# Two attention layers of a fused kernel: output products of heads in pairs, branch steps at set heads, rotation and projection started elsewhere

## What is computed

```python
h = modulate(rmsnorm(x), ...);  z = h @ w_in
q = rope(rmsnorm(z_q) @ w_q_b)                     # 8 heads of 64 + 32 (rotated)
k, v = ...rmsnorm(z_kv) @ w_kv_b...                # context keys first, then tokens
attn = softmax(q k^T / sqrt(96)) v                 # tokens: 512 keys; context: its own 256
conf = silu(layernorm(conv31(a * sigmoid(g)) + b)) # conformer branch, 256 channels
sc   = b_gate * conv3(c_gate * h_gate)             # short convolution branch, 256 channels
y = concat(rmsnorm(attn), rmsnorm(conf), rmsnorm(sc)) @ w_o
x = x + m2 * rmsnorm(y)
x = x + m5 * rmsnorm(relu(h2 @ w1)^2 @ w2)         # h2: modulated x
```

## Time and profile before

| | us |
|---|---|
| median of 3 runs | 1877.29 (1873.92 to 1880.47) |
| the profiled execution, its own time | 1874.17 |
| span of its trace | 1872.4 |
| PE busy | 1680.8 (90%) |
| DVE busy | 1229.1 (66%) |
| ACT busy | 483.0 (26%) |
| POOL busy | 467.5 (25%) |
| granted TensorE clock, mean | 0.955 of full |

### The profile page before, as it was taken

How to read it: one execution, slowest core, us unless ns; L and a number is a source line. 1 busy time by engine, 2 the same in 40 slices (tenths; PEclk the granted TensorE clock), 3 DMA queues, 4 the chain that set the end, 5 groups by cost and what they waited for, 6 DMA issues and landing times.

```text
span 1872.4 us, 26961 instructions
## 1 busy us (share of the span) xinstructions
PE 1680.8 (90%) x10862; PEld 1435.7 (77%) x10862; DVE 1229.1 (66%) x1658; ACT 483.0 (26%) x994; POOL 467.5 (25%) x368
## 2 busy tenths in 40 slices
PE   6888689999787999979988979999999788989997
PEld 6776489999676999958744748888888475679996
DVE  7752458887876888759774364444444696568886
ACT  3323221111351211142345251111011424531111
POOL 2300124443223344312100302121212130134442
PEclk9999799999998999989998989999999898999998
DMA  7445555554465655653200203233323141035561
GB/s 264 147 149 178 226 191 181 179 179 147 168 233 196 203 180 182 186 191 102 83 8 0 81 21 113 90 101 90 100 92 99 35 135 45 22 103 179 177 177 51
DMA packets 69874, 247.26 MB, mean 132 GB/s; under 512 B 7456, under 2 KB 10528, under 8 KB 69664
## 3 DMA queue, kind: packets, MB, share of 16 engines
q1 hardware_dynamic: 69792, 246.18, 40.6%
HBM read 245.10 MB, written 1.05 MB: 131 GB/s over the span
## 4 chain that ended last, share of the span: by engine, by line
PE 60%; DVE 28%; issue 5%; ACT 5%; POOL 1%; DMA 1%; SPq 0%; DVEq 0%; POOLq 0%; ACTq 0%
PE psum L318 13%; PE psum L319 13%; PE psum L320 13%; DVE lo_ring L293 9%; DVE relu L1048 4%; PE psum L334 3%; DVE hid_lo L1050 3%; PE psum L336 3%; PE psum L335 3%; PE psum L1362 2%; DVE c_conf L1592 2%; PE psum L908 1%; DVE x L1012 1%; PE psum L1386 1%; POOL hi_ring L1819 1%
## 5 line engine op out<-in xcount | busy, mean ns | idle before, releaser
L1819 POOL TENSOR_SCALAR hi_ring<-raw_ring 128x1024 fp32r<-128x1024 f32 x364 | 467.3, 1287 | 1377.9 <-PE psum L320 676.5
L293 DVE TENSOR_TENSOR lo_ring<-raw_ring,hi_ring 128x1024 fp32r<-128x1024 f32 x364 | 549.7, 1513 | 95.3 <-POOL hi_ring L1819 62.4
L318 PE MATMUL psum<-x_hi,hi_ring 128*128 128x256 f32 (+1 forms) x1440 | 453.0, 315 | 22.5 <-DVE lo_ring L293 22.5
L319 PE MATMUL psum<-x_lo,hi_ring 128*128 128x256 f32 (+1 forms) x1440 | 447.7, 311 | 0.0
L320 PE MATMUL psum<-x_hi,lo_ring 128*128 128x256 f32 (+1 forms) x1440 | 447.4, 311 | 0.0
L318 PE MATMUL psum<-hid_hi,hi_ring 128*128 128x256 f32 (+1 forms) x1024 | 315.7, 308 | 4.1 <-DVE hid_lo L1050 4.1
L320 PE MATMUL psum<-hid_hi,lo_ring 128*128 128x256 f32 (+1 forms) x1024 | 313.8, 306 | 0.0
L319 PE MATMUL psum<-hid_lo,hi_ring 128*128 128x256 f32 (+1 forms) x1024 | 313.2, 306 | 0.0
L318 PEld LDWEIGHTS psum<-x_hi,hi_ring 128*128 128x128 f32 x1440 | 278.1, 193 | 42.1 <-DVE lo_ring L293 27.4
L319 PEld LDWEIGHTS psum<-x_lo,hi_ring 128*128 128x128 f32 x1440 | 278.1, 193 | 14.2 <-issue 0.2
L320 PEld LDWEIGHTS psum<-x_hi,lo_ring 128*128 128x128 f32 x1440 | 277.8, 193 | 13.8
(11 more groups left out here) (353 smaller groups left out, 1837.8 us busy)
## 6 DMA issues: line engine op xcount, KB each, us to landing
raw_ring<-weights SPq DMA_DIRECT2D x460, 512.0 KB, 3.6
h_const<-hyb_consts SPq DMA_DIRECT2D x1, 1088.0 KB, 11.7
x<-xT SPq DMA_DIRECT2D x1, 1024.0 KB, 6.0
x<-ctxT SPq DMA_DIRECT2D x1, 1024.0 KB, 17.2
outT<-x SPq DMA_DIRECT2D x1, 1024.0 KB, 4.8
shared<-shared_consts SPq DMA_DIRECT2D x1, 398.0 KB, 13.8
par<-params SPq DMA_DIRECT2D x1, 301.5 KB, 6.6
```

Of the source, the lines that this page charges most:

```text
L293: nc.vector.tensor_tensor(lo_ring[:, u % SPLIT_SLOTS, :], raw_ring[:, UNIT_AT[u] % RAW_SLOTS, :], hi_ring[:, u % SPLIT_SLOTS, :].bitcast(F ...
L318: nc.tensor.matmul(bank(u % BANKS, T), w_hi, hi[:, k, 0:T], start=(k == 0), stop=False)
L319: nc.tensor.matmul(bank(u % BANKS, T), w_hi, lo[:, k, 0:T], start=False, stop=False)
L1819: nc.gpsimd.tensor_scalar(hi_ring[:, u % SPLIT_SLOTS, :], raw_ring[:, slot, :], 1.0, 0.0, ALU.mult, ALU.add).then_inc(hi_ready, 1)
```

## The change

Five edits, all in block 2's layers (and one constant that block 1's output projection reads as well).

1. **Heads in pairs.** `out_of(i)` is gone. `out_pair(i)` runs after `scores` in every even iteration for heads i-2 and i-1 together: for each key block one matmul of the even head (partitions 0 to 63), then one of the odd head (partitions 64 to 127), one signal for both. The number of matmuls and their shapes stay. `c_pT` gets four buffers (`c_pT_low`, `c_pT_high`; the second lies over `c_kv`, `c_kr` and `c_q`). DVE's `pair_out` moves one iteration later.
2. **Branch steps per engine.** `PE_STEPS`, `ACT_STEPS` and `DVE_STEPS` name, for each layer, the iterations at which each engine does its steps. PE does them at the head of iteration i as before; ACT and DVE now at its end. The flag `branch_sq` is split in `conf_sq` and `sc_sq`, ACT's `rstd` step in `rstd` and `sc_rstd`, DVE's `silu` step in `scaled` and `sc`. All taps that are left are done in iteration 0.
3. **Early rotation.** The first four rotation matmuls stand in the middle of the last query unit (after its second head) and not behind it; DVE's `rotate(0)` stands ahead of the last six taps of the unit phase and not behind them.
4. **Projection.** `LATE_FIRST` is [6, 7, 4, 5, 0, 1, 2, 3]: the short branch's blocks come first. PE's sum of the attention's squares stands between blocks 7 and 4.
5. **The end on ACT and DVE.** ACT squares three attention blocks, waits for the last output pair, then splits blocks 6, 7, 4, 5 and squares the fourth block among them.

```diff
-    LATE_FIRST = [4, 5, 6, 7, 0, 1, 2, 3]
+    LATE_FIRST = [6, 7, 4, 5, 0, 1, 2, 3]
...
-    STEPS = ["conf_mean", "center", "sums", "rstd", "silu", "again", "last"]
+    PE_STEPS = [{2: ["mean"], 4: ["sums"], 6: ["sc"], 8: ["again"]}, {1: ["mean"], 3: ["sums"], 4: ["sc"], 7: ["again"]}]
+    ACT_STEPS = [{3: ["squares"], 4: ["rstd"], 6: ["sc_rstd", "silu"], 8: ["last"]},
+                 {2: ["squares"], 3: ["rstd"], 4: ["sc_rstd"], 5: ["silu"], 7: ["last"]}]
+    DVE_STEPS = [{0: ["taps"], 2: ["center"], 5: ["scaled"], 7: ["sc"], 9: ["last"]},
+                 {0: ["taps"], 1: ["center"], 4: ["scaled"], 5: ["sc"], 7: ["last"]}]
...
+                if half == 1 and h == 1:
+                    rotations(0)
 
         pe.wait_ge(flag("K_ready"), l + 1)
...
+        rotations(1)
         pe.wait_ge(flag("q_rotated"), 2 * l + 1)
...
-            pe.wait_ge(flag("pT_ready"), L.at + i + 1)
-            r0 = (h % 2) * DV
-            o = psum[r0:r0 + DV, 6, 0:SEQ]
+            pe.wait_ge(flag("pT_ready"), L.at + i + 2)
             for k in range(n):
-                last = nc.tensor.matmul(o, c_v[:, first + k, h * DV:(h + 1) * DV], c_pT[:, i % 2, k * SEQ:(k + 1) * SEQ],
-                                        start=(k == 0), stop=(k == n - 1))
-            last.then_inc(flag("o_head"), 1)
+                for m in range(2):
+                    last = nc.tensor.matmul(psum[m * DV:(m + 1) * DV, 6, 0:SEQ], c_v[:, first + k, (h + m) * DV:(h + m + 1) * DV],
+                                            c_pT(i + m)[:, k * SEQ:(k + 1) * SEQ], start=(k == 0), stop=(k == n - 1))
+            last.then_inc(flag("o_pair"), 1)
...
-            if i in L.hooks:
-                branch_pe(L.hooks[i])
+            for step in PE_STEPS[l].get(i, []):
+                branch_pe(step)
             turned(i)
             if i + 2 < len(L.heads):
                 scores(i + 2)
-            if i:
-                out_of(i - 1)
+            if i and i % 2 == 0:
+                out_pair(i - 2)
+        out_pair(len(L.heads) - 2)
...
+        def block_of(k):
+            if k == LATE_FIRST[2]:
+                attn_sums()
+            pe.wait_ge(x_ready, KT * (L.split + 2) + LATE_FIRST.index(k) + 1)
...
             if i + 2 < len(L.heads):
                 exp(i + 2)
+            for step in ACT_STEPS[l].get(i, []):
+                branch_act(step)
...
+        for i in range(3):
+            attn_sq(i)
+        act.wait_ge(flag("o_pair"), (L.at + len(L.heads)) // 2)
+        act.wait_ge(flag("branch_normed"), 4 * l + 2)
+        branch_hi(LATE_FIRST[0])
+        attn_sq(3)
+        branch_hi(LATE_FIRST[1])
...
+        for i in range(3):
+            next_lo(dve, L.base + L2_IN + i)
+            if i == 2:
+                rotate(0)
+            do_taps(6)
...
-            pair_out(i - 1)
-            do_taps(L.taps)
+            pair_out(i - 2)
+            for step in DVE_STEPS[l].get(i, []):
+                branch_dve(step)
```

More of the change, by code:

```diff
@@ L1373, in turned, with out_pair @@
             last.then_inc(flag("pT_ps"), 1)
-        def out_of(i):
+        def out_pair(i):
             st, h = L.heads[i]
@@ L1497, in branch_act @@
         def branch_act(step):
-            if step == "center":
+            if step == "squares":
                 for i in range(2):
@@ L1551, in l2_act @@
         nc.scalar.activation(rstd[:, 0:T], stat[:, 0:T], ACT.Exp, scale=-0.5).then_inc(flag("attn_rstd"), 1)
-        for k in LATE_FIRST[2:4]:
-            nc.scalar.activation(x_hi[:, k, 0:T], merged(k, T), ACT.Copy).then_inc(split_hi, 1)
         for i, k in enumerate(LATE_FIRST[4:]):
```

93 lines of the change are left out of this document (40 added, 53 removed).

## The result

The changed kernel takes 1883.90 us (median of 5 runs, 1879.86 to 1886.16) against 1877.29 for the kernel before in 5 runs of the same session: **ratio 1.0036, 95% interval 1.0024 to 1.0049**. It is slower by 6.6 us. The forecast was 1877.1, no change that can be told; the sign is the one I gave 0.20. The profiled execution took 1883.90, with a span of 1882.1.

What follows compares the result with a forecast made beforehand. PE was taken to bound 512-key heads, the relay through other engines showing at branch steps. Layer 0 -6.7 + 2.1 = -4.6, layer 1 +2.9 + 1.5 = +4.4, together -0.2: 1877.1 us, range 1866 to 1885.

Steps and rivals of the forecast that it cites:

- the one I gave 0.20: The outcome that the changed kernel is slower than before; chance 0.20, against 0.28 for faster and 0.52 for same.
- The gaps that the sum named: PE idle before `sums` (4.4) and `again` (4) in layer 0, before `sums` (3.1), `sc` (4.05), `again` (3.2) in layer 1.
- The clock's price: Work behind seven PE gaps partly at the lower clock: 1.6 us behind a gap, 10.2 us in all.
- The first rival: PE stays at full clock behind the gaps, or waits come out shorter: -10.4, 1866.9 us; chance 0.28.
- the rule of the Trainium skill: Weight loads overlap running matmuls only where row groups differ; kept as rival that pairs do not overlap: +11.4, 1888.5; chance 0.08.
- the mean ... starts at 1580.5: Layer 1: `mean` starts at 1580.5, after DVE's `rotate(1)`, `normalised(1)`, `top(2)` and last six taps, PE idle over 3 us.
- 978.6: Layer 0: instant reached after the sum, `turned(4)` and `scores(6)` behind the `sums` gap, with 1.6 us of lost clock.
- 999.6: Layer 0: instant reached after `again`, `turned(8)` and `scores(10)`, with 1.6 us of lost clock.
- some 2.7 us each: Layer 0: estimated time for each of the seven 256-key heads left, bound by the relay, not PE.
- -6.7: Layer 0: last output ends at 1019.6 instead of 1026.3, a gain of 6.7 us.
- +2.1 and +1.5: Added projection time in layers 0 and 1, from block 6's and attention block 0's waits; bounds nothing and 3.
- The clock stays low: Rival: the clock has not recovered after a 5.3 us stretch, loss 3.0 a gap: +8.4, 1885.5 us; chance 0.12.

Runs made afterwards that it cites:

- e_old_proj: The changed kernel with the projection's old block order, the attention's sum ahead of the projection and ACT's old end restored; 1878.9 us, ratio 1.0007 to the kernel before.
- e_old_rot: The changed kernel with the rotation of the first four heads moved back behind all query matmuls, on PE and DVE; 1890.4 us, ratio 1.0070 to the kernel before.
- e_mean2: The changed kernel with layer 1's `mean` alone moved back to head 2, on PE and DVE; 1880.1 us, ratio 1.0015 to the kernel before.
- e_serial: The changed kernel with a pair's matmuls run one head after the other, not in turns; 1889.2 us, ratio 1.0066 to the kernel before.
- e_old_steps: The changed kernel with all branch steps of both layers back at the heads of before; 1875.9 us, ratio 0.9990 to the kernel before.
- e_old_l1: The changed kernel with only layer 1's branch steps back at the heads of before; 1872.6 us, ratio 0.9978 to the kernel before.

## Why the prediction was wrong

Instants are counted from the start of the stretch (933.95 and 1558.60 before, which the forecast carries on from; 935.18 and 1559.53 after).

- **The gaps that the sum named were right.** Forecast 4.4, 4.0 (layer 0), 3.1, 4.05, 3.2 (layer 1); measured 4.41, 4.23, 3.07, 3.90, 2.60. A relay time read from one steady head (3.05 and 4.28) carried over to a place that did not exist yet.
- **The clock's price was right in sum, and partly by luck.** The sum held 4.2 and 6.0 us of lost clock, from 1.6 behind one gap; holding the clock up won back 4.1 and 5.8 in the stretches. The first rival, that it doesn't fall, is out. Gap by gap the price was wrong both ways, as the view by stretch of the changed kernel shows (behind `mean` and `again` of layer 0 and `again` of layer 1; the clock is the last but two):

```profile
960.61:965.12 4.51, 4.51 (x17) 1.00 0.00 0
997.57:1003.75 6.18, 6.18 (x13) 0.51 0.00 0
1623.34:1625.31 1.97, 1.97 (x12) 1.00 0.00 0
```

Behind 2.64 us (`mean`, layer 0) and 2.60 us (`again`, layer 1) of idle time the clock was full, and the work took 4.51 and 1.97 us where the forecast had 5.6 and 3.1. Behind `sums` and `again` of layer 0, whose matmuls have 512 columns, it took 7.22 and 6.18 for 6.2 and 4.9; behind `sc` of layer 1 6.11 for 5.3. The length of a gap alone does not tell what follows: 2.03 us was followed by slow work in the kernel before, 2.60 and 2.64 were not here. What else decides stays open.
- **The pairs were right, the rule of the Trainium skill does not hold here** (TensorE: Matmul & The Clock Gate, Part 3): both tiles use all rows and their loads take 137 ns each, but a pair's 16 records run in 1.95 us, forecast 1.88. That is 122 ns a record, less than its load takes, so the loads overlap running matmuls though the rows are the same. The prediction also read that part too narrowly: the Trainium skill gives there a measured speedup of 2.38 for three tiles of 32 columns side by side, which speaks for the pairs. The view of line L1395 in the changed kernel:

```profile
L1395 PEld LDWEIGHTS psum<-c_pT_low,c_v x80: 132/137/137, 965.1 to 1620.1; 128*64 128x64 f32 x80
```

- **The step that failed in layer 1 is "the mean ... starts at 1580.5".** I had DVE as the only bound from `turned(0)` on and let `top(0)` start at 1568.0. But behind the 1.91 us that PE was idle before the first scores, and again behind 2.50 before `turned(0)`, the scores ran at the half clock for part and for all of their time, 5.40 for two heads and 3.62 for one, and DVE waited for each of them, as the rows below show: `top(0)` 1.15 and `top(2)` 0.49 idle. `mean` came 2.5 us later than forecast (24.4 against 21.9), and every later instant carried it: `sums` +2.3, `sc` +2.3; `again` was 3.1 late, by the slow work behind `sc`, and the last output 2.1, since behind `again` the clock was full. I had priced the half clock behind the steps and forgotten it at the start, though the earlier trace rows shows it there: 5.69 behind 4.41. `e_old_proj` runs the same code up to that point and met the clock at full: there `mean` began 27.0 us behind the last value matmul for 28.9 here. So 1.9 of the 2.5 us is the clock's level at the start. Of the rest, 0.3 is DVE's last six taps (2.71 us for 2.45); 0.3 stays unexplained.

The rows are DVE's timeline of the changed kernel, layer 1, `top(0)` and `top(2)`, and the view by stretch of PE's two `scores` ahead of them; the clock is the last but two, 0.68 and 0.50:

```profile
1569.99 1.22 DVE L1686 TENSOR_REDUCE c_soft<-psum 128x2 f32<-128x1024 f32 x1 [1.15 <-PE psum L1372]
...
1579.80 1.23 DVE L1686 TENSOR_REDUCE c_soft<-psum 128x2 f32<-128x1024 f32 x1 [0.49 <-PE psum L1372]
...
1566.48:1571.88 5.40, 5.39 (x8) 2.02 (x8) 3.72 (x8) 0.43 (x1) 0.00 (x0) 0.68 0.01 2
1576.14:1579.76 3.62, 3.62 (x5) 1.01 (x4) 2.95 (x5) 1.02 (x1) 0.00 (x0) 0.50 0.00 0
```

- **The step that failed in layer 0 is the 1.6 us of lost clock behind `sums` and `again`** ("978.6" and "999.6"). `mean` was 1.7 late (25.4 against 23.7). Only 0.49 of it is DVE waiting for scores at the half clock: the first scores ran at the full clock (8 records in 3.60), and `top(0)` was 0.7 late already, behind the rotation and the taps. The full clock behind `mean` gave 1.1 back, so `sums` was 0.6 late; the slow work behind `sums` cost 1.0 more than priced, so `again` was 1.6 late; the slow work behind `again` cost 1.3 more. From there to the end of the outputs it took 20.1 us for 20.0: "some 2.7 us each", an estimate with no row of its own, came out. Last output: -3.7 for -6.7.
- **The projection** was sized at +2.1 and +1.5 and measured +2.7 and +3.4 against before (the earlier trace rows and the stretch ends), 2.4 and 3.1 by `e_old_proj`. The waits were right (1.4 and 0.8 forecast for 1.71 and 0.9 in layer 0; 2.0 and 1.0 for 1.97 and 1.01 in layer 1); left out was that the attention's sum behind them can run at the half clock: in layer 1 3.35 us for 8 records, 3.0 to the next start for 1.8 before. With the new order it did so in the change, in `e_old_rot` (3.53) and in `e_mean2` (3.47), but not in `e_serial`, `e_old_steps` and `e_old_l1` (1.89). And +1.5 does not follow from its own terms: 3.0 less the 1.0 that PE was idle before (0.69 ahead of the attention's sum, 0.32 ahead of a block) is 2.0.
- **Together**: 3.0 (layer 0's heads), 0.6 (its projection), 2.1 and 1.9 (layer 1's) make 7.6 of the 7.7 us between -0.2 and +7.5. None of it is a new mechanism; four terms were short in the same direction, most of it by a clock level that the sum did not carry there. The median moved by 6.6.
- **The rivals.** "The clock stays low" gave 1885.5 and lies near the result, but by another road: behind a gap one pass was slow or none, not two (behind `mean` 1583.95 the second pass took 0.88 and 1.81 to the next start).

## What to carry to other kernels

In an engine that runs in order, a step placed earlier than its input is ready does not start earlier; it only holds back the work behind it. Find when the input is ready (here DVE's last tap), count what can be done until then, and put the step behind that; the placing of every later step of the chain follows from the one before.

When independent work is halved (the pairs), ask first who sets the pace without it: 18.8 us of matmuls came to 2.7 us of time, which is not clear of nothing, because the relay through two other engines was nearly as long. And price TensorE's half clock as a range, at every gap, the first one included: here the work behind gaps of 2.03 to 4.41 us was mostly slow, but behind 2.05, 2.60 and 2.64 us it also ran at the full clock.
